# A 512-token, two-block transformer pass on one core: norm sums reordered, residual written in place, small tables moved

## What is computed

```python
for l in range(2):                                   # first block
    x = x + 0.5 * swiglu(rmsnorm(x, ffn1_norm[l]), ...)          # D_FF = 2816
    h = rmsnorm(x, mix_norm[l])
    x = x + concat([gmlp, shortconv, retention](h @ w_in[l])) @ w_out[l]
    x = x + 0.5 * swiglu(rmsnorm(x, ffn2_norm[l]), ...)
x = rmsnorm(x, final_norm)
...
for layer in range(2):                               # second block
    h = rmsnorm(x, ev_norm or od_norm)
    x = x + (pool + latent attention, or gated linear recurrence)(h)
    x = x + cross_attention(rmsnorm(x, xa_norm_x[layer]), mem)
    x = x + swiglu(rmsnorm(x, ffn_norm[layer]), ...)
return rmsnorm(x, final_norm_2)
```

## Time and profile before

| | |
|---|---|
| median of 3 runs | 3420.61 us (3420.53 to 3421.91) |
| the profiled execution: its own time | 3420.91 us |
| its span, first to last instruction | 3419.5 us |
| TensorE busy | 3299.9 us, 97% of the span |
| VectorE, ScalarE, GpSimd busy | 49%, 29%, 43% |
| mean granted TensorE clock | 0.985 of full |

### The profile page before, as it was taken

One profiled execution on the slowest core, in us unless ns is written; L12 is line 12 of the kernel. 1 busy time (PEld: TensorE's weight loads), 2 busy tenths in 40 slices (PEclk: granted clock), 3 DMA queues, 4 the chain that ended last, 5 costly groups with the idle time before them and its releaser, 6 DMA issues. The chain is left out here.

```text
span 3419.5 us, 36165 instructions
## 1 busy us (share of the span) xinstructions
PE 3299.9 (97%) x14676; PEld 2681.6 (78%) x14676; DVE 1685.3 (49%) x2038; ACT 982.5 (29%) x1264; POOL 1466.6 (43%) x601
## 2 busy tenths in 40 slices
PE   8999999999999999999999979999999979999997
PEld 6888877888888888778888747878888758778886
DVE  4442467544144423675442657465441785474422
ACT  3222332222222223322222353322222453322221
POOL 4444433544454444334444313444444335444442
PEclk9999999999999999999999989999999989999998
DMA  3223322222232233223223202323222223222231
GB/s 135 95 99 99 122 74 80 99 99 99 99 105 94 98 105 119 74 77 105 94 98 105 84 31 83 102 81 105 99 98 97 79 80 105 93 93 96 96 101 65
DMA packets 91413, 321.54 MB, mean 94 GB/s; under 512 B 10224, under 2 KB 12656, under 8 KB 90992
## 3 DMA queue, kind: packets, MB, share of 16 engines
q1 hardware_dynamic: 85392, 309.45, 27.3%
q10 hardware_dynamic: 5856, 9.79, 0.8%
HBM read 317.10 MB, written 2.10 MB: 93 GB/s over the span
## 5 line engine op out<-in xcount | busy, mean ns | idle before, releaser
L1858 POOL TENSOR_TENSOR wlo<-raw,whi 128x1024 fp32r<-128x1024 f32 x588 | 1464.6, 2500 | 1920.3 <-ACT whi L707 1920.3
L325 PE MATMUL bank<-gxh,whi 128*128 128x512 f32 x2848 | 1124.0, 395 | 10.5 <-DVE gxl L1202 5.9
L326 PE MATMUL bank<-gxl,whi 128*128 128x512 f32 x2848 | 1111.1, 390 | 0.0
L707 ACT ACTIVATE whi<-raw 128x1024 fp32r<-128x1024 f32 x588 | 610.2, 1051 | 617.3 <-PE bank L329 596.1
L329 PE MATMUL bank<-gxh,wlo 128*128 128x512 f32 x2848 | 705.9, 390 | 0.0
L325 PEld LDWEIGHTS bank<-gxh,whi 128*128 128x128 f32 x2848 | 536.4, 188 | 129.5 <-DVE gxl L1202 6.7
L326 PEld LDWEIGHTS bank<-gxl,whi 128*128 128x128 f32 x2848 | 536.3, 188 | 117.2 <-issue 6.4
L329 PEld LDWEIGHTS bank<-gxh,wlo 128*128 128x128 f32 x2848 | 536.1, 188 | 111.7
L325 PE MATMUL bank<-f_hh,whi 128*128 128x512 f32 x1056 | 413.6, 392 | 0.0
L326 PE MATMUL bank<-f_hl,whi 128*128 128x512 f32 x1056 | 413.2, 391 | 0.0
L1196 DVE SCALAR_TENSOR_TENSOR xs<-bank,x 128x512 f32<-128x512 f32 x96 | 66.3, 691 | 658.3 <-PE bank L329 642.1
(11 more groups left out here) (317 smaller groups left out, 2620.6 us busy)
## 6 DMA issues: line engine op xcount, KB each, us to landing
raw<-stream SPq DMA_DIRECT2D x588, 512.0 KB, 3.3
m_dk<-decay ACTq DMA_DIRECT2D x2, 1024.0 KB, 6.1
xa_mem<-memT ACTq DMA_DIRECT2D x2, 1024.0 KB, 5.5
outT<-x ACTq DMA_DIRECT2D x1, 2048.0 KB, 7.4
x<-xT ACTq DMA_DIRECT2D x4, 256.0 KB, 5.4
x<-xT SPq DMA_DIRECT2D x4, 256.0 KB, 6.2
m_ct<-cos ACTq DMA_DIRECT2D x2, 256.0 KB, 2.8
m_sn<-sin ACTq DMA_DIRECT2D x2, 256.0 KB, 3.1
```

Of the source, the lines that this page charges most:

```text
L325: pe.matmul(out, seq(hi, k, P), h, start=first and k == 0, stop=False)
L326: pe.matmul(out, seq(hi, k, P), l, start=False, stop=False)
L707: act.activation(M.whi[r][:, :], M.raw[r][:, :], ACT.Copy).then_inc(*S.tick("hi", u))
L1858: pool.tensor_tensor(M.wlo[r][:, :], M.raw[r][:, :], M.whi[r][:, :].bitcast(F32), ALU.subtract).then_inc(*S.tick("lo", u))
```

## The change

It has four parts. (1) At the start ScalarE makes the eight `gxh` first, splits the two units between and behind them, and then makes eight squares into eight separate tiles; VectorE adds them into `acc`; TensorE begins with the first unit and does the norm's sum behind the second one. (2) The last norm is summed on 4 columns (token blocks as the stationary operand, one column of ones moving), its root and reciprocal are 128 x 4, a diagonal times ones spreads it over the partitions, and the output goes out as 8 DMAs of one tile, half on SP's queue. (3) In `residual` the sum is written into `x[m]` itself; ScalarE makes the square and then `gxh[m]`; VectorE keeps `gxl` and `acc`, and in the last stage `gx` isn't made. (4) The small tables are allocated from the far end of SBUF, and `xp0`, `xp1` of `mixer3` stand behind its large tiles.

```diff
-        self.ones, self.ident = sb("ones", P), sb("ident", P)
+        self.ones, self.ident = sb("ones", P, side="right"), sb("ident", P, side="right")
...
-        self.rcol = sb("rcol", RCOL["all"])
+        self.rcol = sb("rcol", RCOL["all"], side="right")
...
+        self.squares = [self.acc, self.sq, self.xs, self.sd, self.R, self.f[0]["a"], self.f[0]["s"], self.f[0]["u"]]
...
     # TensorE
+    def last_norm():
+        b = claim(7, "root", 12)
+        pe.wait_ge(*S.at("acc", 11, KD - 2))
+        pe.wait_ge(*S.at("sq", 11, KD - 1))
+        for n in range(NB):
+            pe.matmul(b[:, n:n + 1], seq(M.acc, n, P), M.ones[:, 0:1], start=True, stop=False)
+            mm = pe.matmul(b[:, n:n + 1], seq(M.sq, n, P), M.ones[:, 0:1], start=False, stop=True)
+        mm.then_inc(*S.tick("sum", 12))
+        b = claim(6, "xo")
+        pe.wait_ge(*S.at("spread"))
+        pe.matmul(b[:, :], M.ones[:, :], M.R[:, :], start=True, stop=True).then_inc(*S.tick("last_rstd"))
...
             project(("gate", f, m), next_bank("a", f, m)[:, :], i if m == 0 else None)
-            if m == 0:
+            if m == 0 and f:
                 norm(i)
             project(("up", f, m), next_bank("u", f, m)[:, :])
+            if m == 0 and not f:
+                norm(i)
...
     # ScalarE, residual
-            act.activation(M.sq[:, :], M.xs[:, :], ACT.Square).then_inc(*S.tick("sq", i, m))
+            act.activation(M.sq[:, :], seq(M.x, m), ACT.Square).then_inc(*S.tick("sq", i, m))
+            if i < F_STAGE[5]:
+                act.activation(seq(M.gxh, m), seq(M.x, m), ACT.Copy, scale=gain(m)).then_inc(*S.tick("gxh", i, m))
...
     # VectorE, residual
-            dve.scalar_tensor_tensor(M.xs[:, :], at_bank("xs", i, m)[:, :], scale, seq(M.x, m), ALU.mult,
+            dve.scalar_tensor_tensor(seq(M.x, m), at_bank("xs", i, m)[:, :], scale, seq(M.x, m), ALU.mult,
                                      ALU.add).then_inc(*S.tick("xs", i, m))
-            dve.wait_ge(*S.at("xs", i, m))
-            dve.tensor_scalar(seq(M.gxh, m), M.xs[:, :], gain(m), None, ALU.mult).then_inc(*S.tick("gxh", i, m))
-            dve.tensor_scalar(seq(M.x, m), M.xs[:, :], 1.0, None, ALU.mult).then_inc(*S.tick("x", i, m))
...
     # VectorE, end
-    rstd(12)
+    dve.wait_ge(*S.at("root", 12))
+    dve.reciprocal(M.sd[:, NB:2 * NB], M.sd[:, 0:NB]).then_inc(*S.tick("rstd", 12))
     dve.wait_ge(*S.at("rstd", 12))
+    dve.wait_ge(*S.at("xs", 11, KD - 1))
+    for n in range(NB):
+        dve.tensor_scalar(seq(M.R, n, P), M.ident[:, :], M.sd[:, NB + n:NB + n + 1], None, ALU.mult).then_inc(
+            *S.tick("spread"))
```

More of the change, by code:

```diff
@@ L679, in mixer3 @@
                  [("y4", k) for k in ALL_Y])
-    fresh()
+    pe.wait_ge(*S.at("fill", "ones"))
     pe.wait_ge(*S.at("masks", "ident"))
@@ L693, in tensor_program @@
     ffn(5)
-    norm(12)
+    last_norm()
 def scalar_program(act, S, M, T_in):
@@ L713, in root @@
         act.wait_ge(*S.at("sum", i))
-        act.wait_ge(*(S.at("rstd", i - 1) if i else S.at("blocks")))
+        act.wait_ge(*(S.at("rstd", i - 1) if i else S.at("acc", -1, KD - 1)))
         act.activation(M.sd[:, :], bank[7][:, :], ACT.Sqrt, bias=EPS, scale=1.0 / D).then_inc(*S.tick("root", i))
     def residual(i, keys):
-        per = len(keys) // KD
+        per, gain = len(keys) // KD, gain_after(M, i)
         for m in range(KD):
@@ L735, in fresh @@
                 *S.tick("gxh_act", m))
-            if m > 1:
-                act.wait_ge(*S.at("fresh_sum", m - 2))
-            act.activation((M.sq, M.xs)[m % 2][:, :], seq(M.x, m), ACT.Square).then_inc(*S.tick("sq", -1, m))
+            if m == KD // 2:
+                split_hi(0)
+        split_hi(1)
+        for m in range(KD):
+            if m == 0:
+                act.wait_ge(*S.at("blocks"))
+            act.activation(M.squares[m][:, :], seq(M.x, m), ACT.Square).then_inc(*S.tick("sq", -1, m))
     def ffn(f):
@@ L1060, in scalar_program @@
         act.dma_start(M.lcols[l][:, :], T_in["lcols"][l]).then_inc(*S.tick("lcols", by=16))
-    for u in range(AHEAD):
-        split_hi(u)
     fresh()
@@ L1073, in scalar_program @@
     ffn(5)
[L1074 to L1078, removed]
+    act.wait_ge(*S.at("sum", 12))
+    act.wait_ge(*S.at("rstd", 11))
+    act.activation(M.sd[:, 0:NB], bank[7][:, 0:NB], ACT.Sqrt, bias=EPS, scale=1.0 / D).then_inc(*S.tick("root", 12))
+    for m in range(0, KD, 2):
+        act.wait_ge(*S.at("xo", m))
+        act.dma_start(T_in["outT"][m * P:(m + 1) * P, :], seq(M.x, m)).then_inc(*S.tick("out_act", by=16))
+    act.wait_ge(*S.at("out_act"))
 class Ring:
@@ L1192, in residual @@
             elif i:
-                dve.wait_ge(*S.at("x", i - 1, m))
+                dve.wait_ge(*S.at("xs", i - 1, m))
             else:
                 dve.wait_ge(*S.at(f"x_tile{m}"))
-            dve.scalar_tensor_tensor(M.xs[:, :], at_bank("xs", i, m)[:, :], scale, seq(M.x, m), ALU.mult,
+            dve.scalar_tensor_tensor(seq(M.x, m), at_bank("xs", i, m)[:, :], scale, seq(M.x, m), ALU.mult,
                                      ALU.add).then_inc(*S.tick("xs", i, m))
-            dve.wait_ge(*S.at("xs", i, m))
-            dve.tensor_scalar(seq(M.gxh, m), M.xs[:, :], gain(m), None, ALU.mult).then_inc(*S.tick("gxh", i, m))
-            dve.tensor_scalar(seq(M.x, m), M.xs[:, :], 1.0, None, ALU.mult).then_inc(*S.tick("x", i, m))
+            if i == F_STAGE[5]:
+                if m < KD - 1:
+                    dve.wait_ge(*S.at("sq", i, m))
+                    dve.tensor_tensor(M.acc[:, :], M.acc[:, :], M.sq[:, :], ALU.add).then_inc(*S.tick("acc", i, m))
+                continue
             dve.wait_ge(*S.at("gxh", i, m))
-            dve.scalar_tensor_tensor(seq(M.gxl, m), M.xs[:, :], gain(m), seq(M.gxh, m).bitcast(F32), ALU.mult,
+            dve.scalar_tensor_tensor(seq(M.gxl, m), seq(M.x, m), gain(m), seq(M.gxh, m).bitcast(F32), ALU.mult,
                                      ALU.subtract).then_inc(*S.tick("gx", i, m))
@@ L1216, in fresh @@
                                      ALU.subtract).then_inc(*S.tick("gx", -1, m))
+        for m in range(1, KD):
+            dve.wait_ge(*S.at("sq", -1, m))
+            if m > 1:
+                dve.wait_ge(*S.at("acc", -1, m - 1))
+            dve.tensor_tensor(M.acc[:, :], M.acc[:, :], M.squares[m][:, :],
+                              ALU.add).then_inc(*S.tick("acc", -1, m))
     def ffn(f):
@@ L1870, in sync_program @@
         sp.dma_start(M.raw[r][:, :], T_in["stream"][u]).then_inc(*S.tick(f"loaded{r}", u, by=16))
+    for m in range(1, KD, 2):
+        sp.wait_ge(*S.at("xo", m))
+        sp.dma_start(T_in["outT"][m * P:(m + 1) * P, :], seq(M.x, m)).then_inc(*S.tick("out_sp", by=16))
+    sp.wait_ge(*S.at("out_sp"))
 def build(nc, T_in, known):
```

24 lines of the change are left out of this document (11 added, 13 removed).

## The result

The changed kernel takes 3386.74 us (median of 4 runs, 3384.22 to 3390.12), the kernel before 3420.57 us on the same chip; the ratio is 0.9903, 95% interval [0.9891, 0.9916]. The profiled execution took 3388.51 us, its span is 3387.3 us, 32.2 us less than before.

A forecast was written before the change was run, and what follows sets the result against it. TensorE, busy 97% of the span, was taken as the bound, through idling, low clock and wide spacing. Gains 8.2 + 9.2 - 0.7 + 10.5 + 6.3 = 33.5 us gave 3387 us, range 3379 to 3401.

The forecast's parts named there:

- Start, 8.2 us: Kernel start: with `gxh` made first, the third unit starts at 27.5 instead of 35.71 us, 8.2 us gained.
- Waits at stages 7 and 10, 9.2 us: Ends of stages 7 and 10: TensorE's waits on the last `gxl` and the low clock behind them go, 9.2 us gained.
- `mixer3`, 0.7 us lost: Stage 8: `mixer3` waits for `acc`, which square, `gxh`, `gxl`, `acc` in line bring later, 0.7 us lost.
- Spacing, 10.5 us: TensorE products in the stages: large moving tiles come to the place of `gxh` modulo 512 bytes, 10.5 us gained.
- Rival 1: Product spacing: a tile's place is not what spaces the products, everything else holds, 3397.5 us; chance 0.17.
- Tail, 6.3 us: Last sum to end of span: 15.3 instead of 21.6 us by shorter norm and tile-wise output, 6.3 us gained.
- Rivals 2 to 5: 2: waits stay, 3396, 0.09; 3: start, tail half, 3394, 0.08; 4: slower, 3437, 0.03; 5: no effect, 3420, 0.03.
- Rival 4: Ends of stages: `gxl` meets GpSimd's subtraction at each, 4.6 us each, so slower, 3437 us; chance 0.03.

The follow-up runs named there:

- e3: The changed kernel with `gxh` made by VectorE again in the residuals, the copy of `xs` to `x` still out: 3386.06 us, ratio 0.9896 to the kernel before.
- e5: The changed kernel with `gxh` on VectorE again and an unused copy of each `x` tile between `gxh` and `gxl`: 3395.24 us, ratio 0.9919.
- e6: The changed kernel with `gxh` on VectorE again and an unused copy of each `x` tile behind the addition to `acc`: 3398.77 us, ratio 0.993.
- e1: The kernel before with part 4 of the change alone (small tables and `xp0`, `xp1` moved): 3411.22 us, ratio 0.9969.
- e2: The changed kernel with part 4 undone, small tables below the stages' tiles again: 3400.16 us, ratio 0.9939 to the kernel before.
- e7: The changed kernel with 64 unused bytes between `gxl` and the weights' tiles, moving weights and stage tiles up: 3437.08 us, one run.
- e4: The changed kernel with the tiles of the six FFNs moved up by 0, 32, 64, 128, 256 and 384 bytes: 3397.06 us, one run.
- e11: The changed kernel with all `gxh` before the first split, last square added on VectorE, `m_ch` at place 0, attention tiles at 192 bytes: 3385.28 us, ratio 0.9889.
- e9: The changed kernel with pads of 16, 48, 96, 160, 192 and 224 bytes below the six FFNs' `f_hh` and `f_hl`: 3404.01 us, one run.

## Why the prediction was right, point by point

The forecast was 3387, the measured median 3386.7. The terms stand nearly as well alone, but the mechanism of the spacing was half wrong, and so was what the prediction took for the clock at the start and in the tail. That the whole came within 0.3 us is luck, since four runs lie between 3384.2 and 3390.1.

- *Start, 8.2 us*: 8.2. First product 12.54 (forecast 12.3), second unit 21.2 (21.0), third unit 27.5 (27.5; its second product starts at 27.73). `gxl[5]` ended at 15.3, the next at 18.1 and the last at 18.75 us, as worked out; one addition was held, as assumed. The clock was not as assumed: full pace was to come at 16 us, and the products stayed 0.43 us apart until 17.8. It cost nothing, since the seventh pair had to wait for its `gxl` in any case.
- *Waits at stages 7 and 10, 9.2 us*: 8.6. The reason given had two halves, and the change shows both: the order on ScalarE puts each subtraction behind `gxl`, so that none of 88 is held, and VectorE, which needs 3.46 us for a tile (3.5 in the prediction) where it took 4.6 before, isn't behind at the last tile. What the prediction missed is that the waits of TensorE hang on the last tile alone, and that less is enough for it. e3 has no such order, `gxl` is held at 7 tiles, and TensorE waits for none; e5 adds one copy of 0.4 us for each tile, and the wait is there again. e6 shows that a copy costs as much at another place, by meeting the subtraction there. Whether the order alone would do, with the copy still on VectorE, no run shows.
- *`mixer3`, 0.7 us lost*: the wait on `acc` grew from 2.9 to 3.4 us (forecast 3.6); e3, with `gxh` on VectorE, has 2.7.
- *Spacing, 10.5 us*: part 4 alone gave 10.6 us of span in e1 and costs 12.3 when it is undone (e2). The FFNs gave 7.1 to 7.3 of it (forecast 7.0). The mechanism as put, the place modulo 512 bytes, was wrong twice: the period is 256, and it is the place relative to the weights (e7). Nor did all large moving tiles come to the place of `gxh`. The 768 products of 256 columns, for which the prediction took a gain of 0.8 us, lost: from 0.113 to 0.118 up to 0.120 us, 1.5 to 5 us together. `m_ch` lost too, 0.227 to 0.233 us: three tiles of 2112 bytes lie below it, 192 bytes more than a multiple of 256, and the tables' 64 had made that round. Other products gained more than taken (those of `m_xh` ran at 0.233 us before and those of `xa_yh` in the first attention at 0.231, not at 0.229), so that the stages without an FFN gave 2.4 us where the prediction's terms for them make 2.7 + 0.8 - 0.7 = 2.8. Rival 1 is ruled out by e1 and e2, and e4 and e7 show the place as the cause. The Trainium skill's page "TensorE: Matmul & The Clock Gate", section Back-to-back issue gap, whose rule sides with rival 1, gives one distance for a width, 0.216 us at 512 columns, and calls it that of an isolated product. The traces here have 0.2267 to 0.2343 us at this one width, so the rule doesn't cover this.
- *Tail, 6.3 us*: 5.7 in the profiled execution, where two misses nearly cancel. The 16 passes took 3.1 us, not 1.8: the first four gaps are 0.11 us, as the 1.8 assumed, the others 0.21, since the granted clock had fallen (0.58 of full on average in the window). The last tile landed 2.2 us after its issue, where 3.1 was taken. But this execution is the exception. Of the eight other runs with these 16 passes, six had 0.11 us throughout at 1.00 of full, e3 and e6 for all but the last passes; their tails take 14.3 to 15.0 us, 6.6 to 7.3 less than before. The clock fell 2.0 us after the last product in the change's execution and 3.0 to 5.3 us after it in the eight. Why it fell when it did is open.

Rivals 2 to 5 didn't happen. Rival 4 had no opening: the cover of 0.2 us between `gxl` and the subtraction is as thin as predicted, but the program's order fixes it, and no `gxl` of a residual is held in the change or in the seven runs that keep this order (e2, e4, e7 to e11). e6 shows the price when another instruction of VectorE stands behind `acc`.

## What to carry to other kernels

When products follow each other without a gap, compare their spacing between stages and look at where the moving operand lies relative to the weights: here 64 bytes cost 1% of a product and most other places 3%, with no idle time shown anywhere, and a small table allocated among large tiles is enough to cause it. Place the operands first, then measure each width by itself, since 256 and 512 columns wanted different places. Where one engine's instruction can hold another's, as GpSimd's subtraction does here, a stall can depend on tenths of a microsecond: read how far apart the two instructions are in the version that works, at every tile, and whether the order of the program fixes this distance (0.24 us at 77 of 88 tiles in the change) or only the timing of this run does (e3). And before a part of a gain is credited to an edit, look at the same stretch in other runs that share its code: the tail of one and the same code took from 14.3 to 15.9 us, most of it by the clock.

## What the runs showed of the hardware that was not expected

- The pace of fp32r products of 512 columns depends on the distance of the moving operand from the weights modulo 256 bytes. For `f_hh` and `f_hl` it is 0.2267 us at 0, 0.2289 at 48 and 64, 0.2333 at 16, 32, 96, 128, 192 and 224, 0.2343 at 160 (e4, e9). For 256 columns it is 0.120 at 0, 0.1187 at 128, 0.1133 at 192 and, in the kernel before, between 0.113 and 0.118 at 64. Why one tile at one place has two paces is open.
- With the weights 64 bytes above `gx` (so -64, or 192) its products took 0.2333 us (e7); those of `f_hh` took 0.2289 at +64 and, as those of `gx`, 0.2333 at 192. The distance isn't symmetric.
- VectorE's copies, scalings and additions of SBUF tiles that start during GpSimd's subtraction end behind it: `gxl` 2.8 to 2.9 us instead of 0.75, `acc` 2.69 instead of 0.69, a copy 2.56 instead of 0.41, `f_hh` 2.5 instead of 0.43. One that reads a bank of PSUM (0.69 us) or a reciprocal (3.35 us) isn't held, and one that already runs when the subtraction starts isn't slowed (`acc` at 2280.44 took 0.68 us).
- At the start the products are 0.43 us apart until 17.8 us, twice the later spacing, while the granted clock of that window (12.54 to 17.80 us) reads 1.00. There the record of the clock doesn't show the low pace, and only the spacing does:

```profile
12.54:17.80 5.26, 5.25 (x12) 1.00 0.55 201
```
